# Relu and square of the lower blocks of quadrant pairs as one VectorE operation behind their last addition, in a two-layer hybrid trunk on one core

## The reference, cut to what matters

```
h = _rmsnorm(x, p['norm_mlp_w'][l]) * (1.0 + sc_m) + sh_m
x = x + gt_m * (jnp.square(jax.nn.relu(h @ p['mlp_w1'][l])) @ p['mlp_w2'][l])
```

## Time and profile before

| | |
|---|---|
| median of three runs | 2658.83 us |
| profiled execution, its own time | 2661.06 us |
| profiled execution, span | 2659.2 us |
| TensorE matmuls (PE) | 2559.3 us busy, 96% |
| weight loads (PEld) | 2391.8 us, 90% |
| VectorE (DVE) | 1530.1 us, 58% |
| ScalarE (ACT) | 972.3 us, 37% |
| GpSimd (POOL) | 693.0 us, 26% |
| mean granted TensorE clock | 0.994 |

### The profile page before, as it was taken

One profiled execution on the slowest core, in us unless ns is written; L12 is line 12 of the kernel. 1 busy time (PEld: TensorE's weight loads), 2 busy tenths in 40 slices (PEclk: granted clock), 3 DMA queues, 4 the chain that ended last, 5 costly groups with the idle time before them and its releaser, 6 DMA issues.

```text
span 2659.2 us, 54007 instructions
## 1 busy us (share of the span) xinstructions
PE 2559.3 (96%) x23060; PEld 2391.8 (90%) x23060; DVE 1530.1 (58%) x2505; ACT 972.3 (37%) x1583; POOL 693.0 (26%) x527
## 2 busy tenths in 40 slices
PE   7998999999999999999999989999999998999998
PEld 6888887989899899999988888889898998999997
DVE  6667625556685726345485675355566957355364
ACT  4251044334422625244342511343344226254352
POOL 2322132332343120220333311223323431211202
PEclk9999999999999999999999999999999999999999
DMA  8110023533343222323331100144332422222222
GB/s 323 40 48 4 3 68 110 158 110 114 102 150 105 80 80 97 105 93 104 138 134 33 41 3 12 61 143 136 115 110 97 161 82 72 73 79 79 81 72 79
DMA packets 74569, 245.59 MB, mean 92 GB/s; under 512 B 8932, under 2 KB 21396, under 8 KB 73184
## 3 DMA queue, kind: packets, MB, share of 16 engines
q1 hardware_dynamic: 71264, 220.32, 24.5%
q0 software_dynamic: 3072, 21.86, 2.2%
HBM read 227.56 MB, written 14.59 MB: 91 GB/s over the span
## 4 chain that ended last, share of the span: by engine, by line
PE 79%; DVE 10%; ACT 5%; issue 3%; DMA 1%; POOL 1%; SPq 0%; DVEq 0%; ACTq 0%; POOLq 0%
PE ps_dense L1068 29%; PE ps_dense L1076 14%; PE ps_dense L1991 5%; PE ps_aux L1068 5%; PE ps_dense L1757 3%; PE ps_dense L1995 2%; PE ps_aux L1521 2%; PE ps_dense L1838 1%; PE ps_aux L1814 1%; PE ps_aux L1507 1%; PE ps_dense L1826 1%; DVE rs L3143 1%; PE ps_aux L1473 1%; ACT flow L2535 1%; ACT w_high L2525 1%
## 5 line engine op out<-in xcount | busy, mean ns | idle before, releaser
L880 POOL TENSOR_TENSOR w_low<-w_ring,w_high 128x256 fp32r<-128x256 f32 (+1 forms) x338 | 536.6, 1605 | 1407.9 <-ACT w_high L2141 1396.3
L2141 ACT ACTIVATE w_high<-w_ring 128x1024 fp32r<-128x1024 f32 x198 | 210.0, 1061 | 365.8 <-PE ps_dense L1068 260.5
L1068 PE MATMUL ps_dense<-z_both,w_high 128*128 128x320 f32 x2048 | 312.4, 310 | 0.0
L1068 PEld LDWEIGHTS ps_dense<-z_both,w_high 128*128 128x128 f32 x2048 | 302.6, 188 | 2.1 <-issue 1.6
L1076 PE MATMUL ps_dense<-h_high,w_high 128*128 128x320 f32 x1024 | 240.7, 316 | 8.0 <-DVE x_res L3165 3.5
L3309 DVE SCALAR_TENSOR_TENSOR x_res<-ps_dense,mod,x_res 128x320 f32<-128x320 f32 (+2 forms) x192 | 72.6, 433 | 292.3 <-PE ps_dense L1068 292.3
L1076 PE MATMUL ps_dense<-h_high,w_low 128*128 128x320 f32 x1024 | 233.1, 309 | 0.0
L1076 PE MATMUL ps_dense<-h_low,w_high 128*128 128x320 f32 x1024 | 232.5, 308 | 0.0
L1068 PE MATMUL ps_dense<-h_high,w_high 128*128 128x320 f32 x864 | 203.8, 317 | 9.4 <-ACT h_high L2188 5.3
L1068 PE MATMUL ps_dense<-h_low,w_high 128*128 128x320 f32 x864 | 188.9, 310 | 0.3 <-DVE h_low L2697 0.3
L1076 PEld LDWEIGHTS ps_dense<-h_high,w_high 128*128 128x128 f32 x1024 | 168.3, 188 | 15.4 <-issue 13.2
(11 more groups left out here) (523 smaller groups left out, 5108.0 us busy)
## 6 DMA issues: line engine op xcount, KB each, us to landing
w_ring<-in_w_mlp SPq DMA_DIRECT2D x128, 512.0 KB, 3.6
w_ring<-in_w_late SPq DMA_DIRECT2D x64, 640.0 KB, 4.0
w_ring<-in_w_gate SPq DMA_DIRECT2D x64, 512.0 KB, 5.4
w_ring<-in_w_in SPq DMA_DIRECT2D x48, 512.0 KB, 3.2
w_ring<-in_w_out SPq DMA_DIRECT2D x16, 512.0 KB, 3.4
w_ring<-in_w_early SPq DMA_DIRECT2D x16, 512.0 KB, 3.3
arena<-in_w_early SPq DMA_DIRECT2D x3, 2048.0 KB, 18.2
arena<-in_dft POOLq DMA_DIRECT2D x2, 2944.0 KB, 12.8
```

Source lines behind the costliest of these rows:

```text
L880: last = g.tensor_tensor(w_low[:, n % 2, k:k + step], ring[:, slot, k:k + step, :], w_high[:, n % 2, k:k + step].bitcast(F32), ALU.subtract)
L1068: last = mm(out[:, s, 0:HALF], w_[:, par_, k, :], x_[:, k, s * HALF:(s + 1) * HALF], start=first, stop=final)
L2141: a(w_high[:, n % 2], ring[:, j, 0:KC, :], ACT.Copy).then_inc(w_high_in.sem, 1)
```

## The change

The Relu and the square of a pair's lower block leave ScalarE. VectorE does both by one instruction, `max(x, 0) * x`, in place over 640 columns, right behind the fifth addition and ahead of the low parts of A22 and S4. It waits for that addition and for the square of the upper block (so that `hid_square` counts in order). ScalarE's `lower_half` is left with `first_product` and the high part. The numbering of `hid_relu` has one step fewer in each pair. The upper blocks, the whole blocks, the products and the loads stay as they are.

```diff
-        hid_relu = signal("hid_relu_and_first_products_kept", 2 * WHOLE + 4 * (PAIRS - WHOLE))
+        hid_relu = signal("hid_relu_and_first_products_kept", 2 * WHOLE + 3 * (PAIRS - WHOLE))
...
-            return hid_relu.nth(l, 2 * WHOLE + 4 * (p - WHOLE) + i)
+            return hid_relu.nth(l, 2 * WHOLE + 3 * (p - WHOLE) + i)
...
             def lower_half(l, p, following=None):

-                act.wait_ge(*quadrant_in(l, p, 5))
-                a(hid_sq[:, 1], hid_sq[:, 1], ACT.Relu).then_inc(hid_relu.sem, 1)
-                hidden_square(l, 2 * p + 1, relu_in(l, p, 4))
                 if following:
                     first_product(l, following)
                 hidden_high(l, 2 * p + 1)
...
                 dve.wait_ge(*product_done(l, p, 7))
                 v.tensor_tensor(lower[:, 0:HALF], lower[:, 0:HALF], q_r, ALU.add).then_inc(quad_in.sem, 1)
+                dve.wait_ge(*quadrant_in(l, p, 5))
+                dve.wait_ge(*hid_square.nth(l, 2 * p + 1))
+                v.scalar_tensor_tensor(out=lower, in0=lower, scalar=0.0, in1=lower, op0=ALU.max, op1=ALU.mult)\
+                    .then_inc(hid_square.sem, 1)
                 prepare("A22", "S4")
```

## The result

The changed kernel is slower. Its median is 2680.88 us (2678.52 to 2682.97, four runs) beside 2659.24 us for the kernel before (four runs), and the ratio, run against run, is 1.0072 with a 95% interval of 1.0057 to 1.0086: 15 to 23 us. The profiled execution spans 2676.7 us, 17.5 more than before.

The account below looks back on a forecast made before the run. The prediction took a loop through VectorE and ScalarE to pace the MLP's pairs, with TensorE waiting at product 5. Six groups of four (14.5 us) plus group 0 (1.6) gave 16.1 us, so a median of 2674.9, range 2666 to 2680.

Parts of the forecast that it names:

- The direction and the mechanism: In the MLP's pairs, VectorE's added operation delays ScalarE's copy of the first product; slower beyond 0.2%, chance 0.90.
- The duration: VectorE's new 128x640 operation takes 0.82 us, as a row of the same form does.
- Reading one tensor as both operands: Rival: VectorE's new operation reads its shared operand once and takes 0.494 us; 9.7 us slower, 2668.5, chance 0.06.
- a slower operation: Rival: VectorE's new operation takes 0.885 us or a little more; 17.4 us and up, 2676 to 2680, chance 0.06.
- The displacement of A22's low part: In VectorE's queue, A22's low part starts 0.865 us later behind the new operation.
- The tie: ScalarE's and VectorE's branches into the copy of the first product are equally long to within 0.05 us.
- 0.81 us per transition: From pair to pair in a group, the copy of the first product shifts by 0.865 minus 0.05 us.
- Half clock: Rival: TensorE's longer gaps at product 5 drop its clock to 1.2 GHz; 35 us at 20 places, 2710, chance 0.01.
- Group ends: In a group's last pair the last low part comes some 0.8 us earlier; nothing waited, nothing is gained.
- The sum: Over both layers, 14.5 us from six groups of four and 1.6 from group 0: 16.1 us slower.

Follow-up runs that it names:

- clean relief: Kernel before, with ScalarE's Relu and square of the pairs' lower blocks left out and VectorE's queue untouched: ratio 1.0001.
- addition alone: Kernel before, ScalarE keeping Relu and square, plus one 128x640 operation on VectorE behind the fifth addition: 2687.85 us, ratio 1.0092.
- the double: Changed kernel with a second 128x640 VectorE operation (a Relu in place) ahead of the new one: 2697.24 us, ratio 1.0129.
- second profile of the changed kernel: Changed kernel run again without any edit, beside the two reordered kernels: 2675.22 us, ratio 1.0057 to the kernel before.
- third order: ScalarE's and VectorE's queues reordered in both kernels: changed kernel 2650.36 us, ratio 0.9954; kernel before 2652.90 us, 0.9965.

## Why the prediction was right, point by point

**The direction and the mechanism** were right: two branches lead into the copy of the first product, the change empties the one and lengthens the other, and idle time behind the merge doesn't help. The clean relief (1.0001), the addition alone (period 14.34) and the double (15.20) show each half by itself.

**The duration** of the new operation: 0.82 predicted from a row of the same form, 0.82 to 0.83 measured. Reading one tensor as both operands gives nothing, so that rival is out, and so is a slower operation. The displacement of A22's low part was 1.255 - 0.39 = 0.865 predicted and 1.26 - 0.39 = 0.87 measured. ScalarE has 38.2 us less to do and not 41, since its rows overlap and an overlap counts once in the busy time: in the stretch of the earlier trace rows the Relu starts at 2348.87, 0.09 us before the high part ahead of it ends (2348.24 + 0.72).

**The tie** was mis-sized, in the term "0.81 us per transition". I put VectorE's branch 0.05 us ahead, with a wake-up of 0.04 us taken from another pair of engines. The copy starts 0.09 us behind the low part's end in the changed kernel (2346.11 to 2346.20) and in the clean relief (2335.47 to 2335.56), where only that branch is left. By the earlier trace rows it was 2350.28 to 2350.37 before too: VectorE's branch was not ahead, and the shift is 0.86 in full, which would be 1 us more over 20 transitions.

**Half clock**, given 0.01, is the weakest step. The reasoning was that a gap of 2.31 us had left the clock at 1.00, so gaps of 1.5 to 1.75 would, and that the trace shows no fall. In the changed kernel it fell behind three gaps: 2.29 us in the first pair of group 0 in layer 1, 1.75, and 2.13; the first is the very gap that hadn't lowered it before. One row of a gap that did no harm was no proof. And the trace of the kernel before does show a fall, outside the pairs, between the layers (TensorE's row, then the stretch around it):

```profile
1344.71 0.76 PE L1068 MATMUL ps_dense<-h_high,w_high 128*128 128x320 f32 x2 [1.51 <-ACT h_high L2188]
```

```profile
1344.00:1348.00 4.00, 2.88 (x10) 2.48 (x11) 4.00 (x5) 3.94 (x6) 2.35 (x1) 0.61 0.00 0
```

The price was overrated for these places as well. From 2364.16 to the next product 5 at 2378.17 it is 14.01 us, where 84 matmuls at the upper level take 0.25 + 83 x 0.147 = 12.45: the fall cost some 1.6 us. Into the fourth pair TensorE has some 0.8 us of waiting to lose first, so 0.8 are left. In the first pair of group 0 TensorE still waits 0.93 us at the next product 5 (0.45 before), so the loop through VectorE takes it whole. Group 1 to group 2 in layer 1 took 3.3 us more than before (2333.64 to 2444.64, against 2325.22 to 2432.95), where group 2 to group 3, with no lowered clock, took 2.5 (to 2555.06, against 2540.90); the last group has another such place. That is 0.8 us each at two places, not 35 us in all. The Trainium skill, "TensorE: Matmul & The Clock Gate", Part 1, lets the clock follow a window that runs on its own and doesn't start with a gap, and two gaps of 1.74 us with different outcomes in one execution agree with that. It also wants the array idle through a window for a fall, and names a longer idle time than any gap here had; the rows decide, and they don't show what tells the gaps with a fall from those without.

**Group ends** were right: in the last pair ScalarE's last high part now starts 0.03 us behind the new operation, and TensorE had no wait there to lose:

```profile
2385.02 0.74 ACT L2530 ACTIVATE z_both<-flow 128x640 fp32r<-128x640 f32 x1 [0.59 <-DVE flow L3470]
```

**The sum:** 16.1 us forecast. Between the first additions and behind the last one the first profile holds 8.04 + 9.30 + 0.66 = 18.0 us more. By the first additions, the 20 transitions are 16.8 of them: 6.1 at the eight into a second pair (0.76 each), 5.5 at the six into a third and 5.2 at the six into a fourth. The other 1.2 lie between a fourth pair and what follows, 0.66 each behind the two places with a lowered clock that cost time. So the sum came as near as it did partly by luck: the tie put at 0.05 and the lowered clock put at nothing made it too small by 1.0 and some 1.3 to 1.6, and the transitions into second pairs, taken to cost as much as the others, made it too large. Those vary: in the second profile of the changed kernel they hold 3.7 us where the first has 6.1. Why they do is open, and so is a step of 0.35 us into the third pair of the last group (14.69 in the one profile and 14.70 in the other, in place of 14.34).

The median of 2680.88 is 0.9 above the upper end of the range, 2680; the ratio times the median shown before, 2658.83 x 1.0072, is 2678.0 and inside. The ratios put the change at +19 and +15 us in two series; 16.1 lies between.

## What to carry to other kernels

The chain that ended last names one branch at each merge, the later one. Before work is moved off it, look up everything else that the merge's instruction waits for and how long before it that ended: here the two ended within 0.1 us of each other, the move bought nothing, and the work, put on the other branch, cost its full length. Idle time of the receiving engine counts only if it lies ahead of the step that the chain takes from it: the same operation cost 0.86 us a transition, 0.35 further down the queue, and nothing that the profiles show in a third order, for which both queues were rearranged.

## What the runs showed of the hardware that was not expected

- A wait with a marker and no work between two VectorE operations costs 0.36 us (0.75 from start to start in place of 0.39), nearly half of a 640-wide operation.
- TensorE's granted clock can fall behind gaps of 1.74 to 2.3 us between long runs of matmuls, and need not. The gap of 2.3 us (2.28 to 2.31) in the first pair of layer 1 is in eight of the ten profiles: the clock fell behind it in six (to 0.72 over 6 us in the changed kernel) and stayed at 1.00 in the kernel before and in the clean relief. In layer 1 it fell behind three of seven gaps over 1.5 us in the first profile of the changed kernel, two of four in the second, and all four of 2.31 to 2.40 us in the kernel with two operations.
- ScalarE's operation that reads PSUM started 0.09 us behind VectorE's end (2346.11 to 2346.20 in the changed kernel), one that reads SBUF 0.03 us behind it (2384.16 + 0.83 to 2385.02).
